# The first block's norms: a stage's first unit multiplied without the token factor

## The reference, cut to what matters

```python
def rms_norm(x, g):
    xf = x.astype(jnp.float32)
    y = xf * lax.rsqrt(jnp.mean(xf * xf, axis=-1, keepdims=True) + RMS_EPS)
    return y.astype(x.dtype) * g.astype(x.dtype)

def swiglu(xn, w_in, w_out):
    gu = xn @ w_in
    return (jax.nn.silu(gu[..., :D_FF]) * gu[..., D_FF:]) @ w_out

def first_block(x, ...):
    h = x
    for i in range(2):
        if i == 0:   # three groups of queries, keys, values; 8 heads of 128
            h = h + dilated_attention_mixer(rms_norm(h, attn_norm[0]), ...)
        else:        # causal 4-tap convolution of q and k, gates, 8 heads
            h = h + mlstm_mixer(rms_norm(h, mlstm_norm[0]), ...)
        h = h + swiglu(rms_norm(h, ffn_norm[i]), ffn_w_in[i], ffn_w_out[i])
    return rms_norm(h, final_norm)
```

## Time and profile before

| | before |
|---|---|
| median of 3 runs | 3011.59 us (3007.96 to 3014.16) |
| the profiled execution: time / span | 3009.2 us / 3007.4 us |
| PE busy in the span | 2895.8 us (96%) |
| DVE / ACT / POOL busy | 1998.6 (66%) / 1197.1 (40%) / 351.6 (12%) us |
| chain that ended last | PE 85%, DVE 8%, ACT 4% |
| mean granted clock | 0.987 of full speed |

### The profile page before, as it was taken

The page is one execution under the profiler, slowest core; times in us unless marked ns, Lnnn a source line. Parts: engine busy times, 40 slices in busy tenths (PEclk is TensorE's granted clock), DMA queues, the critical chain, the costliest instruction groups (busy, mean ns, idle before and its releaser), DMA issues.

```text
span 3007.4 us, 42747 instructions
## 1 busy us (share of the span) xinstructions
PE 2895.8 (96%) x17730; PEld 2508.4 (83%) x17730; DVE 1998.6 (66%) x3252; ACT 1197.1 (40%) x1953; POOL 351.6 (12%) x545
## 2 busy tenths in 40 slices
PE   7999999989989989999999999999999999998998
PEld 7999998889977768888864788888888888876998
DVE  6776777668745557777643776777777667654665
ACT  5444444554444434223322632223234222443543
POOL 0000000000113220000122100001010000243000
PEclk9999999999999999999999999999999999999999
DMA  6444675347755523544464255553545545565453
GB/s 217 155 154 141 211 238 184 122 155 245 238 114 84 83 56 121 173 154 155 134 189 119 84 161 161 161 168 119 163 132 166 155 155 167 128 109 88 137 186 127
DMA packets 362275, 451.88 MB, mean 150 GB/s; under 512 B 12656, under 2 KB 332432, under 8 KB 362080
## 3 DMA queue, kind: packets, MB, share of 16 engines
q1 hardware_dynamic: 326976, 329.89, 33.8%
q0 software_dynamic: 34944, 118.65, 16.7%
q10 hardware_dynamic: 160, 0.59, 0.1%
HBM read 438.67 MB, written 1.05 MB: 146 GB/s over the span
## 4 chain that ended last, share of the span: by engine, by line
PE 85%; DVE 8%; ACT 4%; issue 1%; DMA 1%; POOL 1%; DVEq 0%; ACTq 0%; POOLq 0%
PE ps L1155 24%; PE ps L1157 24%; PE ps L1156 24%; PE ps L1333 2%; PE ps L1176 2%; PE ps L1177 2%; PE ps L1178 2%; DVE lo L1662 1%; PE ps L1320 1%; DVE lo L1665 1%; DVE NB L1696 1%; ACT hi L1365 1%; PE ps L1308 1%; PE ps L1288 1%; PE ps L1188 1%
## 5 line engine op out<-in xcount | busy, mean ns | idle before, releaser
L1155 PE MATMUL ps<-XN,hi 128*128 128x256 f32 (+1 forms) x3120 | 1037.6, 333 | 40.2 <-DVE XN L1682 10.1
L1156 PE MATMUL ps<-XN,hi 128*128 128x256 f32 (+1 forms) x3120 | 1021.2, 327 | 0.0
L1157 PE MATMUL ps<-XN,lo 128*128 128x256 f32 (+1 forms) x3120 | 1020.8, 327 | 0.0
L1155 PEld LDWEIGHTS ps<-XN,hi 128*128 128x128 f32 x3120 | 599.5, 192 | 115.4 <-issue 13.9
L1157 PEld LDWEIGHTS ps<-XN,lo 128*128 128x128 f32 x3120 | 599.7, 192 | 48.7
L1156 PEld LDWEIGHTS ps<-XN,hi 128*128 128x128 f32 x3120 | 600.2, 192 | 47.3
L1741 DVE CUSTOM_DVE_ANT_0 MX<-MW,C 128x1024 bf16<-128x1024 f32 x384 | 479.5, 1249 | 114.5 <-DMA MW<-in_mod_w 107.7
L1662 DVE TENSOR_TENSOR lo<-raw,hi 128x1024 fp32r<-128x1024 f32 (+1 forms) x313 | 382.5, 1222 | 244.6 <-ACT hi L1365 243.3
L1365 ACT ACTIVATE hi<-raw 128x1024 fp32r<-128x1024 f32 (+1 forms) x313 | 326.1, 1042 | 429.0 <-PE ps L1157 428.9
L1155 PE MATMUL ps<-H,hi 128*128 128x512 f32 (+1 forms) x1072 | 380.7, 355 | 0.0
L1665 DVE TENSOR_TENSOR lo<-raw,hi 128x1024 fp32r<-128x1024 f32 (+1 forms) x313 | 380.2, 1215 | 0.0
(11 more groups left out here) (239 smaller groups left out, 3400.1 us busy)
## 6 DMA issues: line engine op xcount, KB each, us to landing
raw<-in_mlp_w SPq DMA_DIRECT2D x128, 1024.0 KB, 5.3
MW<-in_mod_w POOLq DMA_DIRECT2D x192, 512.0 KB, 3.8
raw<-in_ffn_w_in SPq DMA_DIRECT2D x44, 1024.0 KB, 5.1
raw<-in_attn_w_in SPq DMA_DIRECT2D x36, 1024.0 KB, 4.9
raw<-in_na_wqkv SPq DMA_DIRECT2D x24, 1024.0 KB, 5.2
raw<-in_ffn_w_out SPq DMA_DIRECT2D x16, 1024.0 KB, 6.0
raw<-in_mlstm_w_in SPq DMA_DIRECT2D x12, 1024.0 KB, 5.1
raw<-in_cv_w SPq DMA_DIRECT2D x12, 1024.0 KB, 6.6
```

The lines of the kernel that those rows point to most:

```text
L1155: e.matmul(out, whi, xhi, start=first, stop=False)
L1156: e.matmul(out, whi, xlo, start=False, stop=False)
L1157: i = e.matmul(out, wlo, xhi, start=False, stop=last)
```

## The change

Five things change, all in the first block.

1. **Rows times the norm's weight, early.** Behind each residual and its square, `gained` makes `XN` = X times the norm weight of the coming stage, high half by ACT (L1443 of the new kernel) and low half by DVE (L1723). It is put into that half of `XN` which the present products do not read; the normed rows proper go to the other half.
2. **The first unit of each stage reads these (`xg`)**, before the factor is known, and its two banks are multiplied by the factor when read out (`normed_late`, DVE, L1730) in place of ACT's copy. For the first feed-forward unit ACT's Silu follows in place. The ones products stand behind the third k of that unit.
3. **`norm_late`** issues the split of the second unit ahead of the factor, then the factor, then scale and rest as before. All other units of the stage read the normed rows, as before. The feed-forward's second unit, the up unit, becomes `outer`.
4. **mLSTM:** the gate columns stand behind the first convolved unit rather than ahead of it.
5. **The start:** parameters and the first unit are loaded ahead of the constants and positions, and two units are split ahead of the factor.

The core of the diff:

```diff
     def ahead_of_all(self):
         if self.known is not None:
             self.bring(0)
+            self.do("begin_rest")
             self.splits()
-            self.unit_next = 1
+            self.bring(1)
+            self.unit_next = 2
...
                 for i, t in enumerate(group):
                     self.do("product", j, t, k, kt, banks[i], x, k == 0, k == kt - 1)
+                if x[0] == "xg" and k == 2:
+                    self.flush()
...
+    def norm_late(self, gain, at):
+        self.splits()
+        used, s = self.xn_used[1], self.rstd(S)
+        for k in range(KT + 2):
+            if k < KT:
+                self.do("scale", s, k, S, gain, None, used, at)
+            if k >= 2:
+                self.do("rest", s, k - 2, S, None, at)
...
         self.do("residual", self.norms, j, n, gate, b, u, last)
         if last:
             self.square(j, n)
+            if self.next_gain:
+                self.gained(j, *self.next_gain)
...
-        p.linear("ffn_w_in", layer, 0, KT, j * 256, 256, x, evac_g, outer=j == 0)
-        p.linear("ffn_w_in", layer, 0, KT, DFF + j * 256, 256, x, evac_u)
+        p.linear("ffn_w_in", layer, 0, KT, j * 256, 256, x if j else xg, evac_g, outer=j == 0)
+        p.linear("ffn_w_in", layer, 0, KT, DFF + j * 256, 256, x, evac_u, outer=j == 0)
...
     convolved(0)
+    gates()
     convolved(2)
...
+        e.dma_start(m.PV[:, :, :], T["params"]).then_inc(*sig["pv"].says("params"))
+
+    def begin_rest():
         e.dma_start(m.cst[:, :], T["consts"][:, 0:m.width]).then_inc(*sig["cst"].says("consts"))
-        e.dma_start(m.PV[:, :, :], T["params"]).then_inc(*sig["pv"].says("params"))
...
+    def gain(s, k, gain, at, used):                                   # ACT
+        w.wait_ge(("x", s, k), used, "params")
+        e.activation(m.XN[:, 0, k, at:at + S], m.X[:, k, 0:S], ACT.Copy, scale=gain_of(m, gain, k, 0)).then_inc(
+            *act.says(("xghi", s, k)))
...
+    def gain(s, k, gain, at, used):                                   # DVE
+        w.wait_ge(("xghi", s, k))
+        e.scalar_tensor_tensor(out=m.XN[:, 1, k, at:at + S], in0=m.X[:, k, 0:S], scalar=gain_of(m, gain, k, 0),
+                               in1=m.XN[:, 0, k, at:at + S].bitcast(F32), op0=ALU.mult, op1=ALU.subtract).then_inc(
+            *dve.says(("xg", s, k)))
+
+    def normed_late(out, b, u, s, *names):
+        w.wait_ge(("acc", b, u), ("rstd", s))
+        e.tensor_tensor(out, m.ps[b][:, 0:S], m.RS[:, 0:S], ALU.mult).then_inc(*dve.says(("free", b, u), *names))
```

More of the change, by code:

```diff
@@ L1405, in scale @@
             w.wait_ge(("scaled", s, k, 0))
-            e.activation(m.XN[:, 0, k, 0:n], tmp[:, 0:n], ACT.Copy).then_inc(*act.says(("xnhi", s, k, 0)))
+            e.activation(m.XN[:, 0, k, at:at + n], tmp[:, 0:n], ACT.Copy).then_inc(*act.says(("xnhi", s, k, 0)))
             return
@@ L1424, in conditions, with dil_qk @@
         e.preload_act_table_set(LNEXP)
-    def dil_qk(pair, g, which, t, b, u):
+    def dil_qk(pair, g, which, t, b, u, late):
+        if late is not None:
+            return
         w.wait_ge(("acc", b, u), ("dil_mixed", 2 * pair - 3) if pair >= 2 else None)
@@ L1453, in dil_mix, with ffn_gate @@
         e.activation(m.XN[:, 0, h, S:512], m.ps[b][:, 0:S], ACT.Copy).then_inc(*act.says(("mohi", "dil", h)))
-    def ffn_gate(layer, j, t, b, u):
+    def ffn_gate(layer, j, t, b, u, late):
+        if late is not None:
+            w.wait_ge(("sgx", layer, t))
+            e.activation(m.SG[:, 0, t, :], m.SG[:, 0, t, :], ACT.Silu).then_inc(*act.says(("sg", layer, 0, t)))
+            return
         w.wait_ge(("acc", b, u), ("hf", layer, 2 * j - 3) if j >= 2 else None)
@@ L1509, in ml_close, with ml_qk @@
         e.activation(m.XN[:, 0, h, S:512], m.HS[:, h % 2, :], ACT.Copy).then_inc(*act.says(("mohi", "ml", h)))
-    def ml_qk(k, b, u):
+    def ml_qk(k, b, u, late):
+        if late is not None:
+            return
         w.wait_ge(("acc", b, u))
@@ L1631, in scalar @@
     go_through(p, {
-        "tables": tables, "split": split, "square": square, "rstd": rstd, "scale": scale,
+        "tables": tables, "split": split, "square": square, "rstd": rstd, "scale": scale, "gain": gain,
         "square_part": square_part, "rstd_part": rstd_part, "scale_part": scale_part, "cv_out_part": cv_out_part,
@@ L1666, in split, with dil_qk, ffn_gate, ml_qk @@
             *low.says(("lo", j, 1), ("spent", j)))
-    def scale(s, k, n, gain, shift, unit):
+    def gain(s, k, gain, at, used):
[6 more added lines that the diff above has]
+        e.tensor_tensor(out, m.ps[b][:, 0:S], m.RS[:, 0:S], ALU.mult).then_inc(*dve.says(("free", b, u), *names))
+    def dil_qk(pair, g, which, t, b, u, late):
+        if late is not None:
+            normed_late(m.QK[:, pair % 2, g, which, t, :], b, u, late, ("qk", pair, g, which, t))
+    def ffn_gate(layer, j, t, b, u, late):
+        if late is not None:
+            normed_late(m.SG[:, 0, t, :], b, u, late, ("sgx", layer, t))
+    def ml_qk(k, b, u, late):
+        if late is not None:
+            normed_late(m.CB[:, k, 3:3 + S], b, u, late, ("ml_cb", k))
+    def scale(s, k, n, gain, shift, unit, at=0):
         tmp = (m.TN, m.SQ)[k % 4 // 2][:, k % 2, :]
@@ L2066, in vector @@
     go_through(p, {
-        "begin": begin, "split": split, "scale": scale, "rest": rest, "residual": residual,
+        "begin": begin, "split": split, "gain": gain, "dil_qk": dil_qk, "ffn_gate": ffn_gate, "ml_qk": ml_qk,
+        "scale": scale, "rest": rest, "residual": residual,
         "scale_part": scale_part, "rest_part": rest_part, "residual_part": residual_part,
```

68 lines of the change are left out of this document (42 added, 26 removed).

## The result

| | before | changed |
|---|---|---|
| median | 3011.49 us (8 runs, 3007.96 to 3014.16) | 3019.51 us (8 runs, 3016.28 to 3025.43) |
| ratio, 95% interval | | 1.003 (1.0021 to 1.0039) |
| profiled execution: time / span | 3009.2 / 3007.4 us | 3022.99 / 3021.2 us |

It is slower by 8.0 us, where I forecast 6.6 us faster (3005). Later it was timed again beside other kernels: 3019.12 us (9 runs), ratio 1.0025 (1.0015 to 1.0034).

The account below looks back on a forecast made before the run. PE bounds the kernel, 85% of the chain of waits. Gains 4.4 + 0.9 + 1.0 + 2.3 less 2.1 for clock falls take 6.5 us off the profiled 3009.2, 2.4 under the median: 3005 us, range 2999 to 3012.

Parts of the forecast that it names:

- The start: Attention's first units: fourth unit's product at 37.5 us instead of 41.98, gain 4.4 us (bounds 2.5 to 5.8).
- the sum: Whole kernel: four gains less 2.1 us for new clock falls, 6.5 us off, giving 3005 us.
- Between the `ffn_w_out` units there is room: First feed-forward's output units, ahead of mLSTM: only the ones products delay the factor; no cost counted.
- The output projections: Projections ahead of both feed-forwards: a residual round through ACT of 6.15 us, where PE's unit takes 5.76.
- The feed-forwards: Third units of both: gains of 0.9 and 2.3 us, each behind a new wait of 2.3 us.
- mLSTM: `outer_gate`'s unit 1.0 us earlier (bounds -1.5 to 2), despite 3.9 us of PE idle at the second convolved unit.
- Nothing in the sum: Conditioning steps slide to later tiles, hidden under PE's units: counted at zero, bounds -1.5 to 1.5 us.
- a change far behind 850 us: Sign of being wrong: a stage far behind 850 us changing by more than 2 us.
- slower: Rival, chance 0.08: the way between residuals through ACT takes longer, PE waits in the projections; 3018 us.

Follow-up runs that it names:

- e3: Kernel before with only the change's start (late attention norm, new load order, two units split ahead); 3007.67 us, ratio 0.9987.
- e1: Changed kernel with the first up units calling `beside` again, so the conditioning steps stand where they stood before; 3013.61 us, ratio 1.0009.
- f1: e1 with rows times weight made behind the next unit's split instead of between the residuals; 3004.24 us, ratio 0.9974.
- g1: f1 with the conditioning steps slid as in the changed kernel; 3008.16 us, ratio 0.999.
- e2: Kernel before with only the conditioning steps slid, by the first up units not calling `beside`; 3010.8 us, ratio 0.9998.
- p1: e2 with two extra ones products ahead of the norm between the blocks, meant to delay the second block; 3009.49 us, ratio 0.9997.
- p2: Kernel before with two extra ones products ahead of the norm between the blocks, conditioning steps not slid; 3009.53 us, ratio 0.9997.
- k3: f1 with credit taken away ahead of the last long mlp stage, so the last neighbourhood layer has three conditioning steps; 3009.21 us, ratio 0.9989.
- k1: Changed kernel with its two missing credits given back in the second feed-forward, so steps are in place for the second block; 3015.79 us, ratio 1.0014.
- k2: Changed kernel with credit given back ahead of the second block's long mlp stages, leaving two steps in the last neighbourhood layer; 3019.52 us, ratio 1.003.

## Why the prediction was wrong, point by point

**The start: right.** Ones products 10.72 (forecast 10.5), first product 16.90 (16.5), fourth unit 37.83 (37.5), a wait of 1.96 us before it (1.0 to 2.4). The product stands 4.15 us earlier, of which a fall of the clock gave 1.6 back. The 2.6 us left are 1.2 less than the 3.8 of the sum. e3 shows the gain in the total.

**"Between the `ffn_w_out` units there is room": wrong, the step that failed first.** I had worked out the round through ACT for the output projections and then costed it at nothing here, where a unit's residuals come every third unit only. But the split of the next unit stands behind those residuals on DVE, behind a conditioning step of 2.4 us as well. 2.26 us from residual to split became 4.21, the cover was gone, and PE waited 4.0 us in e1 (3.5 in the changed kernel), where the sum had nothing; the ledger of the changed kernel lost 4.4. f1 takes the cause away and no such wait is left. With the same cost in the two output projections, the place of the rows is worth 9.4 us (3013.6 to 3004.2).

**The output projections: right in kind, too small.** I forecast a round of 6.15 us; residuals of the changed kernel stand 6.48 us apart, for the second residual came 1.9 us after the first, not 1.63. By timeline on its DVE:

```profile
281.42 0.42 DVE L1804 TENSOR_TENSOR X<-ps,X 128x256 f32<-128x256 f32 x1
282.72 0.67 DVE L1723 SCALAR_TENSOR_TENSOR XN<-X,PV,XN 128x256 fp32r<-128x256 f32 x1 [0.89 <-ACT XN L1443]
283.31 0.41 DVE L1804 TENSOR_TENSOR X<-ps,X 128x256 f32<-128x256 f32 x1
...
287.90 0.42 DVE L1804 TENSOR_TENSOR X<-ps,X 128x256 f32<-128x256 f32 x1
```

**The feed-forwards: waits right, gains mis-sized.** Waits of 1.05 and 2.02 us where I had 1.0 and 2.3. But I took the first one's gain as 0.9, and against the start's lead it was nothing (-2.59 to -2.34 us); the second's was 1.2, not 2.3 (+2.26 to +1.02). A fall of the clock followed both, 1.6 and 2.2 us, where I had counted 0.5 x 1.5 each. Together they lost 2.8 us (1.84 and 1.0 in the ledger) instead of winning 1.7: 4.5 us of the miss, as much as `ffn_w_out`'s.

**mLSTM: right.** A wait of 3.96 us at the second convolved unit (3.9), and 1.4 us won (1.0).

**"Nothing in the sum": wrong, the second step that failed.** I bounded the slid steps at 1.5 us. Putting them back is worth 5.5 us in the changed kernel (3019.1 to 3013.6) and 3.9 in f1 against g1, by my estimate 2.4 and 0.8 of them through the clock. I named a change far behind 850 us as what would prove me wrong, and 12.4 us of it came in the profiled execution. Against the kernel before, 13.7 us more of that stretch ran at half clock (17.1 and 23.9 us in the two neighbourhood layers, 10.2 and 17.1 before), which by the same estimate is 6.8 us of the 12.4. The sum counted falls of the clock in the first block only. e2, and p1 against p2, show no cost of the slide with the first block of before. k3 finds 5.0 us behind 2200 us, k1 wins 3.3 back ahead of the second block, which is not clear of noise, and k2 could not win it back by the count of steps in layer 3. So three pairs point one way (e1 with the changed kernel, f1 with g1 at the edge of noise, f1 with k3) and two show nothing. What failed is the bound of 1.5 us and the silence on the clock; why the slid steps cost something with the new first block and nothing with the old one stays open.

**The sum.** By the ledger at 882 us the changed kernel is 1.4 us late where I had it 6.5 early, 7.9 us off: the start 1.2, the two feed-forwards 4.5, `ffn_w_out` 4.4, less 0.4 that mLSTM won over its forecast and 1.9 from 731 to 882, where the kernel before had more time at half clock (6.8 us against 3.4). Another 12.4 us came behind it. That makes 20.3 us between two profiled executions; of the medians it is 14.5, for the one of the changed kernel was 3.5 us over its median and the one of the kernel before 2.3 under it.

The two steps that the experiments undo, 9.4 + 5.5 = 14.9 us, come to the miss of 14.5, and f1, without both, took 3004.2 where I forecast 3005. This is in part luck. The forecast had charged 3.4 us for the slow rounds in the output projections (3.3 - 0.9 and 3.3 - 2.3), which f1 no longer has, so that my terms would give f1 3001.6.

Of the rivals, "slower" named the round through ACT that is too long, and its 3018 lies nearest to the 3019.5 measured (its own terms, 14.5 us against the gain of 6.5, give 3019.5). That is luck too: it asked for a way through ACT some 0.8 us longer, and from residual to residual it was 0.3 us longer (1.9 against 1.63), the multiplication taking 0.49 us where I had taken 0.42; it wanted PE to wait 2 us in each of six rounds, and in attention's projection PE waited 0.6 us in all for a split. It needed no slow instruction, only the split standing behind the round.

## What to carry to other kernels

In this kernel work put between two instructions of a tight sequence cost the round trip to the other engine (0.88 us idle and the instruction, at each residual), and the one who paid was the split behind it in the queue. So put new preparation behind the next unit's split, never between residual and split. Where an estimate finds a slow round in one stage, apply it to every stage that has the same sequence before calling any of them roomy. And when a term rests on "hidden", ask what else lies in the same gap (here a conditioning step of 2.4 us), and look for executions' own spread, and for the time at half clock in each, before trusting one profile's last 5 us.

## What the runs showed of the hardware that I had not expected

**The length of a wait does not settle whether the clock falls.** f1 and g1 have the same instructions up to 300 us, and in both PE waits 3.44 us for the fourth unit. This is g1, at full clock, 2.4 GHz, in the next 3.4 us (31 matmuls):

```profile
37.91 0.36 PE L1197 MATMUL ps<-XN,hi 128*128 128x256 f32 x1 [3.44 <-DVE lo L1717]
```

```profile
38.60:42.00 3.40, 3.40 (x31) 3.40 (x30) 3.33 (x7) 1.58 (x3) 0.00 (x0) 1.00 0.60 181
```

and this is f1, with 19 at half:

```profile
37.77 0.35 PE L1200 MATMUL ps<-XN,hi 128*128 128x256 f32 x1 [3.44 <-DVE lo L1720]
```

```profile
38.60:42.00 3.40, 3.40 (x19) 3.40 (x18) 3.33 (x7) 1.05 (x2) 0.00 (x0) 0.52 0.63 195
```

So a wait of 2 to 3.5 us costs itself and, in some executions, 1.6 us more (e1 waits 2.02 us there and keeps its full clock, the changed kernel 1.96 us and does not). The Trainium skill, TensorE: Matmul & The Clock Gate, section HAM oscillation, describes a kernel whose waits for a DMA, of some 3 to 5 us, send the clock back every single time. Here a wait of that length did so in f1 and not in g1, and the four waits of the changed kernel above did it too, three of them at 1.96 to 2.02 us, shorter than the page's.

**Executions of one kernel differ by more than many effects.** The kernel before ranged from 3004.9 to 3016.1 us in 29 runs beside g1; f1's profiled execution took 3009.4 us, 5.2 over its median, with 5.4 us lost in layer 3 alone (-5.1 to +0.2 in the ledger), of which 5.1 is time at half clock (27.3 us there against 17.1).
